# Moving work between the engines' orders at three stage boundaries of a two-block kernel, with part of a mask copied by ScalarE

## The reference, cut to what matters

```python
def even_layer(h, ...):
    u = rmsnorm(h, norm_g)
    z_a, xs, Bm, Cm, dt_f, dt_b, z_b, glu_v, glu_g = split_cols(u @ w_in, IN_E_SIZES)
    y_a = ssd_mixer(xs, Bm, Cm, dt_f, dt_b, z_a, ...)
    y_b = conformer_conv(glu_v, glu_g, dw_w, dw_b, ln_g, ln_b) * silu(z_b)
    return h + concatenate([y_a, y_b]) @ w_out

# ssd_mixer: xs, B, C go through a 5-tap convolution and silu; then in each direction
#   y = (C B^T * exp(differences of cumulated log a), lower triangle) @ (x * dt)
# then y_f + y_b + D * x, times silu(z_a), rmsnorm
```

## Time and profile before

| | us |
|---|---|
| median of 3 runs | 2369.8 |
| lowest, highest | 2365.5, 2371.14 |
| the profiled execution | 2370.42 |
| its span, first to last instruction | 2368.7 |
| mean granted clock of TensorE in it | 0.987 |
| busy: TensorE, VectorE, ScalarE, GpSimd | 2292.1, 1568.5, 1091.0, 453.4 |

### The profile page before, as it was taken

One profiled execution on the slowest core, in us unless ns is written; L12 is line 12 of the kernel. 1 busy time (PEld: TensorE's weight loads), 2 busy tenths in 40 slices (PEclk: granted clock), 3 DMA queues, 4 the chain that ended last, 5 costly groups with the idle time before them and its releaser, 6 DMA issues.

```text
span 2368.7 us, 43312 instructions
## 1 busy us (share of the span) xinstructions
PE 2292.1 (97%) x18679; PEld 2211.6 (93%) x18679; DVE 1568.5 (66%) x2517; ACT 1091.0 (46%) x1572; POOL 453.4 (19%) x315
## 2 busy tenths in 40 slices
PE   6999999999999999999999899988999999999998
PEld 6999999999999999999999788988999998888998
DVE  3546666554565567599999899895846456666564
ACT  4334555544544455344334565453535344444443
POOL 6210000000000000078877001750000012221000
PEclk9999999999999999999999999999999999999999
DMA  7756444555565565545556355564555565555552
GB/s 230 179 109 164 147 147 147 176 169 182 174 189 185 184 190 162 162 147 163 178 176 190 117 173 163 156 206 126 178 171 167 175 181 143 169 156 157 184 185 95
DMA packets 378894, 393.99 MB, mean 166 GB/s; under 512 B 12677, under 2 KB 371589, under 8 KB 378261
## 3 DMA queue, kind: packets, MB, share of 16 engines
q1 hardware_dynamic: 373984, 383.22, 53.2%
q0 software_dynamic: 2976, 6.63, 1.9%
q10 hardware_dynamic: 1744, 1.38, 0.2%
HBM read 388.85 MB, written 5.95 MB: 167 GB/s over the span
## 4 chain that ended last, share of the span: by engine, by line
PE 86%; DVE 10%; ACT 1%; issue 1%; DMA 1%; POOL 0%; SPq 0%; ACTq 0%; DVEq 0%
PE ps L421 26%; PE ps L423 25%; PE ps L422 25%; DVE ps L1704 3%; PE ps L2470 1%; PE ps L2399 1%; PE ps L2447 1%; PE ps L2459 1%; DVE wlo L374 1%; PE ps L2213 1%; DMA raw<-in_w_in_dram 1%; PE ps L2230 1%; PE ps L2132 1%; DVE arena L1672 0%; DVE op_lo L500 0%
## 5 line engine op out<-in xcount | busy, mean ns | idle before, releaser
L421 PE MATMUL ps<-op_hi,whi 128*128 128x256 f32 (+1 forms) x5440 | 1572.7, 289 | 12.5 <-POOL wlo L374 6.7
L423 PE MATMUL ps<-op_hi,wlo 128*128 128x256 f32 (+1 forms) x5440 | 1554.1, 286 | 0.0
L422 PE MATMUL ps<-op_lo,whi 128*128 128x256 f32 (+1 forms) x5440 | 1551.6, 285 | 0.0
L367 ACT ACTIVATE whi<-raw 128x1024 fp32r<-128x1024 f32 (+1 forms) x688 | 721.9, 1054 | 920.3 <-PE ps L423 893.2
L421 PEld LDWEIGHTS ps<-op_hi,whi 128*128 128x128 f32 x5440 | 1030.4, 189 | 37.4 <-issue 32.3
L423 PEld LDWEIGHTS ps<-op_hi,wlo 128*128 128x128 f32 x5440 | 1031.0, 190 | 0.0
L422 PEld LDWEIGHTS ps<-op_lo,whi 128*128 128x128 f32 x5440 | 1028.9, 189 | 0.4
L374 DVE TENSOR_TENSOR wlo<-raw,whi 128x1024 fp32r<-128x1024 f32 x552 | 669.0, 1227 | 497.1 <-ACT whi L367 496.3
L374 POOL TENSOR_TENSOR wlo<-raw,whi 128x1024 fp32r<-128x1024 f32 x136 | 334.5, 2471 | 1092.6 <-ACT whi L367 1092.2
L1704 DVE SCALAR_TENSOR_TENSOR ps<-arena,param_cols,ps 128x257 f32<-128x257 f32 (+6 forms) x448 | 183.4, 488 | 0.5
L752 POOL TENSOR_TENSOR arena<-arena 128x256 f32<-128x256 f32 x64 | 62.6, 998 | 277.8 <-DMA arena<-bias_by_column 277.8
(11 more groups left out here) (361 smaller groups left out, 1489.2 us busy)
## 6 DMA issues: line engine op xcount, KB each, us to landing
raw<-in_e_w_in_dram SPq DMA_DIRECT2D x96, 1024.0 KB, 5.4
raw<-in_w_in_dram SPq DMA_DIRECT2D x84, 1024.0 KB, 5.2
raw<-in_o_w_in_dram SPq DMA_DIRECT2D x64, 1024.0 KB, 6.1
raw<-in_e_w_out_dram SPq DMA_DIRECT2D x32, 1024.0 KB, 5.4
raw<-in_w_out_dram SPq DMA_DIRECT2D x16, 1024.0 KB, 5.3
raw<-in_w_ple_gate_dram SPq DMA_DIRECT2D x16, 1024.0 KB, 5.3
raw<-in_o_w_out_dram SPq DMA_DIRECT2D x16, 1024.0 KB, 5.3
arena<-cum_rows SPq DMA_DIRECT2D x16, 544.0 KB, 6.4
```

What stands on the lines that cost most here:

```text
L367: nc.scalar.activation(half_view(whi[c % 2], c, n), half_view(raw[c % RING], c, n), ACT.Copy).then_inc(hi_ready, 1)
L421: nc.tensor.matmul(o, wh, xh, start=(i % cpp == 0 and k == 0), stop=False)
L422: nc.tensor.matmul(o, wh, xl, start=False, stop=False)
L423: mm = nc.tensor.matmul(o, wl, xh, start=False, stop=(i % cpp == cpp - 1 and k == 7))
```

## The change

Three places in the order of the engines' work are changed, and two computations of the scan are written another way.

- bc to zb2: ScalarE does the last Silu of C and the first half of the next split ahead of the first two seg_exp. VectorE does seg(0), half of a split, the masks, seg(1), both weighs, the other half, seg(2).
- z2 to oa: VectorE does `ya_lo(0)` before z2's last pair, then the last product, `ya_lo(1)`, and the split of oa's chunk 1 after all four groups; `conv31(15, 2)` comes after the sums. ScalarE does the last `ya_hi` before the last squares.
- In oa: `total_pe` comes after chunk 1 in place of 0, `cf_sum` after 2 in place of 1, the totals of squares after chunks 5 and 7 in place of 3 and 5, and the steps behind shift by a chunk. `ya_scale` goes into the first `oa_add`.
- `masked_cb` keeps only the six products. The five copies are made by ScalarE (`cb_rest`), which waits for them (`cb_masked`); the first weigh of each group waits for the copies (`cb_rest`).
- The exponents of the meta positions of both directions are made by one tensor_tensor add at the beginning of seg and one tensor_tensor min at its end, on a strided view (`meta_ends`), in place of two tensor_scalar. The columns move for it.

```diff
@@ -116,7 +116,7 @@
...
 SSD_COLS = [(0, 0, 0, T2, 528), (0, 1, P, T2, 384), (1, 0, 0, P, 256), (1, 1, 0, 2 * P, 0),
-            (1, 2, 0, T2, 800), (0, 2, 2 * P, T2, 1072)]
+            (1, 2, 0, T2, 816), (0, 2, 2 * P, T2, 800)]
 META_CUT = 512 - T2
@@ -256,6 +256,10 @@
...
         XNAT = ar(q, 3, S1)
+
+        def meta_ends(sg):
+            return sg[0:META, 800:1088].rearrange("p (a n) -> p a n", n=META)[:, 0:18:17, :]
+
         assert q + 768 <= 19264
@@ -1044,17 +1048,29 @@
...
                 nc.scalar.activation(sg[:, 0:P], rw[:, 1, 0:P], ACT.Exp, bias=LNB[:, 1, SH + n:SH + n + 1])
-                nc.scalar.activation(sg[0:META, 800:1056], rw[0:META, 1, 0:2 * P], ACT.Exp, bias=LNB[0:META, 2, SH + n:SH + n + 1])
-                ins = nc.scalar.activation(sg[0:META, 1056:1088], sg[0:META, 1056:1088], ACT.Exp)
+                nc.scalar.activation(sg[0:META, 816:1072], rw[0:META, 1, 0:2 * P], ACT.Exp, bias=LNB[0:META, 2, SH + n:SH + n + 1])
+                ins = nc.scalar.activation(meta_ends(sg), meta_ends(sg), ACT.Exp)
                 ins.then_inc(S("seg_exp"), 1)
-            seg_exp(0)
-            seg_exp(1)
+            def cb_rest(G):
+                act.wait_ge(S("cb_masked"), G + 1)
+                for d, st, lo, hi, at in SSD_COLS[0:4]:
+                    r = (lo + P, hi) if d == 0 else (lo, P * st)
+                    if r[0] < r[1]:
+                        nc.scalar.activation(CBM[:, at + r[0] - lo:at + r[1] - lo], ps[:, 6 + st, r[0]:r[1]], ACT.Copy)
+                at = SSD_COLS[4][4]
+                nc.scalar.activation(CBM[0:META, at + META_CUT:at + 2 * P], ps[0:META, 7, T2:T2 + 2 * P - META_CUT], ACT.Copy)
+                nc.scalar.activation(CBM[0:META, at:at + META_CUT], ps[0:META, 6, T2:T2 + META_CUT], ACT.Copy).then_inc(S("cb_rest"), 1)
+
             act.wait_ge(acc_free, ST["zb2"].p0)
...
             s = ST["zb2"]
-            halves(act, "act", s.c0 + 2)
+            split_hi(act, s.c0 + 2, 0)
+            seg_exp(0)
+            cb_rest(0)
+            seg_exp(1)
+            split_hi(act, s.c0 + 2, 1)
@@ -1081,6 +1097,8 @@
...
                     seg_exp(2 * pr + 2)
+                if pr % 2 == 1 and pr < 2 * SG - 1:
+                    cb_rest(G + 1)
             act.wait_ge(acc_free, ST["z2"].p0)
@@ -1107,17 +1125,17 @@
...
             side("z2", z2_evac, pre=z2_pre, extra=zb2_silu)
+            ya_hi(2, ST["z2"].end)
+            ya_hi(3, ST["z2"].end)
             ya_square(6)
             ya_square(7)
-            ya_hi(2, ST["z2"].end)
-            ya_hi(3, ST["z2"].end)
             cf = NORM["cf"]
...
             def cf_steps(i):
-                if i == 0:
+                if i == 1:
                     act.wait_ge(S("factor_ms"), 5)
                     nc.scalar.activation(YRS, YRS, ACT.Sqrt).then_inc(S("factor_rt"), 1)
-                i -= 1
+                i -= 2
                 if i in (1, 3):
@@ -1798,16 +1816,21 @@
...
                     dve.wait_ge(S("y_psum"), n - 2 + SEED)
-                for d, st, lo, hi, at in SSD_COLS:
-                    m = P if st < 2 else META
+                both = [w[0:META, 2, :].rearrange("p (d h) -> p d h", d=2)[:, :, n:n + 1].to_broadcast([META, 2, META]) for w in (LNB, LND)]
+                v.do(V.tensor_tensor(meta_ends(SEG[n % 3]), ROWS[0:META, h // 2, :, h % 2, 2 * P:T2], both[0], ALU.add))
+                for d, st, lo, hi, at in SSD_COLS[0:4]:
+                    m = P
                     f = (P * st, P * st + m) if hi - lo > P + META else (lo, hi)
                     col = SH * d + n
-                    ins = V.tensor_scalar(SEG[n % 3][0:m, at + f[0] - lo:at + f[1] - lo], ROWS[0:m, h // 2, d, h % 2, f[0]:f[1]],
+                    V.tensor_scalar(SEG[n % 3][0:m, at + f[0] - lo:at + f[1] - lo], ROWS[0:m, h // 2, d, h % 2, f[0]:f[1]],
                                           LNB[0:m, st, col:col + 1], LND[0:m, st, col:col + 1], ALU.add, ALU.min)
-                ins.then_inc(S("seg_ready"), 1)
+                v.sync()
+                V.tensor_tensor(meta_ends(SEG[n % 3]), meta_ends(SEG[n % 3]), both[1], ALU.min).then_inc(S("seg_ready"), 1)
...
                 dve.wait_ge(S("seg_exp"), n + 1)
+                if n % 4 == 0:
+                    dve.wait_ge(S("cb_rest"), n // 4 + 1)
                 for m, lo, hi in ((P, 0, 800), (META, 800, 1088)):
@@ -1830,22 +1853,19 @@
...
                         o = T2 - META_CUT
-                        if d == 1:
-                            v.do(V.tensor_copy(CBM[0:n, at:at + META_CUT], ps[0:n, 6, T2:T2 + META_CUT]))
-                            v.do(V.tensor_copy(CBM[0:n, at + META_CUT:at + 2 * P], src[:, o + META_CUT:o + 2 * P]))
-                    elif hi - lo > n:
-                        r = (lo + n, hi) if d == 0 else (lo, P * st)
-                        v.do(V.tensor_copy(CBM[0:n, at + r[0] - lo:at + r[1] - lo], src[:, r[0]:r[1]]))
                     dlo = P * st
...
                 v.sync()
+                dve.sem_inc(S("cb_masked"), 1)
             seg(0)
+            split_lo(dve, "dve", ST["zb2"].c0 + 2, 0)
+            masked_cb(0)
             seg(1)
-            halves(dve, "dve", ST["zb2"].c0 + 2)
+            weigh(0)
+            weigh(1)
+            split_lo(dve, "dve", ST["zb2"].c0 + 2, 1)
             seg(2)
-            masked_cb(0)
-            weigh(0)
             for pr in range(2 * SG):
@@ -1854,7 +1874,8 @@
...
                     split_lo(dve, "dve", ST["zb2"].c0 + pr + 3, 0)
-                weigh(2 * pr + 1)
+                if pr > 0:
+                    weigh(2 * pr + 1)
                 if pr < 2 * SG - 1:
@@ -1876,19 +1897,27 @@
...
                     sum_pair(dve, 0, i // 2 - 2, T2)
-                if i == 15:
-                    ya_lo(0)
-                    ya_lo(1)
-
-            def conv_z2(i):
-                if i < 15:
+
+            s = ST["z2"]
+            for i in range(15):
+                z2_pre(i)
+                halves(dve, "dve", s.c0 + i + 2)
+                if i % 2 == 1:
+                    pair_wait(dve, s, i // 2)
+                    z2_times(i // 2, (s.p0 + i // 2) % 2)
+                if i < 14:
                     conv31(12 + i // 4, i % 4)
-
-            side("z2", z2_times, extra=conv_z2, pre=z2_pre)
+            ya_lo(0)
+            pair_wait(dve, s, 7)
+            z2_times(7, (s.p0 + 7) % 2)
+            ya_lo(1)
+            sum_pair(dve, 0, 5, T2)
             ya_lo(2)
             ya_lo(3)
+            halves(dve, "dve", s.end + 1)
             sum_pair(dve, 0, 6, T2)
             sum_pair(dve, 0, 7, T2)
+            conv31(15, 2)
@@ -1898,6 +1927,8 @@
...
             def oa_add(j, par):
+                if j == 0:
+                    ya_scale()
                 V.tensor_tensor(YT, ps[:, pairof(par), 0:T2], YRS.unsqueeze(1).to_broadcast([P, 2, T2]), ALU.mult).then_inc(acc_free, 1)
@@ -1913,11 +1944,10 @@
...
                 if i == 0:
-                    ya_scale()
                     conv31(15, 3)
...
                     dve.sem_inc(S("conv31_state"), 1)
-                i -= 1
+                i -= 2
                 if i == 1:
@@ -1929,7 +1959,7 @@
...
                     cf_half(1)
-                if i == 3:
+                if i == 4:
                     cf_half(2)
@@ -2406,12 +2436,12 @@
...
                 stream_pe(pe, "oa", NT=T2, need="ya", lo=i, hi=i + 1)
-                if i == 0:
+                if i == 1:
                     total_pe(pe, 0, 4, T2)
-                if i == 1:
+                if i == 2:
                     pe.wait_ge(S("conv31_state"), 2)
                     T.matmul(ps[:, 5, 0:T2], ones[:, :], CSUM[:, :], start=True, stop=True).then_inc(S("cf_sum"), 1)
-                for g in {3: (0, 1), 5: (2, 3)}.get(i, ()):
+                for g in {5: (0, 1), 7: (2, 3)}.get(i, ()):
                     pe.wait_ge(norm_half, 4 * cf + g + 1)
```

## The result

The changed kernel takes 2343.5 us (median of four runs, 2343.3 to 2344.1) beside 2367.7 us for the kernel before (four runs, 2365.2 to 2371.1). The ratio is 0.990, with a 95% interval of 0.988 to 0.991. The forecast was 2350.5 with a range from 2344 to 2360: the sign was right, the gain was 24 us by these medians where 19.3 was forecast, and the time fell half a microsecond outside the range. Against the profiled execution of before on which the sum was made, 2370.42 us, the changed kernel's 2343.57 is 26.9 us less. I account for these 26.9. A spell of half clock is a stretch in which TensorE's granted clock is 0.50.

The account below looks back on a forecast made before the run. TensorE, carrying 86% of the chain, was taken as the bound, so only its waits and low clock could pay. 7.3 - 0.8 + 12.8 = 19.3 us off 2369.8 gave 2350.5 us, range 2344 to 2360.

Parts of the forecast that it names:

- the rounds: Scan's seven four-head rounds after the first, 19.15 us each: copies' chain through ScalarE costs +0.12 us a round, 0.8 lost.
- Joint 1: Entry into the scan: with the Silu first, TensorE starts the first B-C product 7.1 us sooner; 7.3 us in all.
- what is late next: Entry of the scan: after the Silu, the wait on conv31_state, so TensorE starts at 1321.1 instead of 1328.2.
- The second term: Entry of the scan: 0.2 us gained from a shorter stay at the low clock.
- -0.8: Seven scan rounds: 0.8 us lost, bounds 0 to 3.5 us lost.
- Joint 2: From scan to z2: only its clock time changes; zero change taken, bounds -3.9 and +2 us.
- Rival B: Scan to z2: weigh runs before GpSimd's split, saving 2.1 us of stall and 1.8 of half clock; 2346.6 us, chance 0.17.
- the prediction's own objection to B: Scan to z2: the seg behind the weigh may be held by GpSimd's split instead.
- Joint 3: From z2 to oa: two more chunks done before the total of squares, 11.9 us plus 0.9, together 12.8 us.
- the 0.9 us that the chain was to give: In oa: VectorE has the sum of squares ready at 1624.3 where it was ready at 1625.2.
- the prediction's own signs of being wrong: Scan rounds' period above 19.7 us, or two chunks not won from z2 to oa.
- rival A: Copies' chain costs its upper end, 3.5 us, and z2 to oa gives only 8: gain 11, 2359 us, chance 0.17.

Follow-up runs that it names:

- meta_only: Kernel before with only the meta exponents of both directions made in two tensor operations, masks' copies still on VectorE, old order: 2367.1 us, ratio 0.999.
- copies_only: Kernel before with only the masks' five copies moved to ScalarE, meta exponents and order as before: 2370.6 us, ratio 1.000.
- before_again: The kernel before, unchanged, run once more for a second trace: 2368.0 us.
- joint1_only: Kernel before with only the new order at the entry of the scan (Silu first), masks' copies and meta exponents as before: 2361.9 us, ratio 0.997.
- joint3_only: Kernel before with only the new order from z2 to oa and the totals one or two chunks later: 2355.6 us, ratio 0.994.
- order_only: Kernel before with only VectorE's and ScalarE's new order from z2 to oa, TensorE's totals in their old places: 2370.1 us, ratio 1.001.
- shift_only: Kernel before with only the totals and their steps one or two chunks later in oa, order of z2's end as before: 2358.9 us, ratio 0.995.
- scan_only: Kernel before with both scan edits, copies by ScalarE and meta exponents in two operations, entry in the old order: 2364.2 us, ratio 0.998.
- tab_late: Changed kernel with GpSimd's table load moved behind z2's chunk 3: 2340.8 us, ratio 0.988 of before.
- ya_first: Changed kernel with ya_lo(1) ahead of z2's last pair: 2344.6 us, ratio 0.989 of before.
- best: Changed kernel with GpSimd's table load behind z2's chunk 3 and the masks' copies back on VectorE: 2340.4 us, ratio 0.988 of before.
- fill_last: Kernel before with seven idle products put in front of the last round's transposes, where TensorE waited: 2366.3 us.

## Why the prediction was right and wrong

The time fell outside the range mainly because two terms of the sum were wrong in kind: the rounds, taken to be bound by TensorE, and the half clock around the scan's last round, put at zero change.

**Joint 1** was right in its term (7.1 us, to 0.1) and in what is late next, the convolution. The second term, 0.2 us for the clock, was too small: the first rows ran faster and the stall of the second group shrank, 0.9 us more.

**The rounds** are the step that failed in its mechanism: "where it is negative TensorE is the bound and nothing is gained". I took TensorE to be the bound at 19.15 us since it was busy 19.97 of 20 us and showed no wait. It was not. The chain through VectorE, which I had set out with a slack of 0.05 us, was the bound, by 0.15 us a round, in pieces too small to be listed as waits; meta_only and copies_only show it from both sides. The larger piece stands at the y product. A weigh and the y product that uses it, before and after:

```profile
1376.50 1.34 DVE L1813 TENSOR_TENSOR arena<-arena 128x800 f32<-128x800 f32 x2
...
1377.98 2.25 PE L2399 MATMUL ps<-arena 128*64 128x272 f32 x24
```

```profile
1367.32 1.34 DVE L1836 TENSOR_TENSOR arena<-arena 128x800 f32<-128x800 f32 x2
...
1368.97 2.25 PE L2429 MATMUL ps<-arena 128*64 128x272 f32 x24
```

Before, the product starts 0.14 us after the weigh's end and 0.32 after the last multiplication; after, 0.31 and 0.22. So 0.10 us was VectorE's there, and 0.05 at the transposes, which started 0.05 us after y_tile's end and now start 0.17 after it. The terms were nearly right: masks and copies took 1360.00 to 1362.04, 2.04 us against 1.96 (forecast 2.03 at the low end), a seg 1.23 against 1.44 (a saving of 0.2 where I took 0.15). But two segs, not one, stand ahead of the y product that ends last, and a shorter chain pays. So -0.8 was +1.05. The copies took 0.81 us, from 1361.12 to 1361.93, and weigh started 0.11 later; the rows had given 0.84. My estimate of 1.01 us from the Trainium skill, ScalarE: Activation LUTs, section What ACT_TABLE_LOAD costs, is 0.20 above the measurement.

**Joint 2** had the largest error for its size: "I leave it at zero change". Its waits did stay (1.90 and 1.87 us against 2.06 and 1.86). Rival B came half true: the weigh does run first, at its usual 1.35 us, but GpSimd's split then holds the seg behind it, as the prediction's own objection to B had it, and the stall stays. In the kernel before, too, such a split held a seg, 3.74 us from 1457.39 for six operations that take 1.51 in other rounds. But the 3.0 us of half clock that followed the two waits in the profiled execution were not a fixed part of the kernel. In all seven traces with a last-round wait of 2.06 us or more (before, before_again, joint1_only, joint3_only, copies_only, order_only, shift_only) a spell followed; in the six with 1.6 to 1.9 us (after, scan_only, meta_only, tab_late, ya_first, best) none did. That is a count and no rule: behind GpSimd's wait of 1.9 us, the same in all, the spell came in seven of twelve traces (before, joint3_only, shift_only, scan_only, meta_only, ya_first, fill_last) and not in five (before_again, joint1_only, copies_only, order_only, after). I had bounded the term by -3.9 us, but gave that corner only to rival B, with a chance of 0.17, and only together with the stall.

**Joint 3** was right in mechanism and, partly by luck, nearly in size: 13.4 us to the total of squares against 12.8. TensorE waited 2.2 us there, as forecast (about 2). But VectorE's chain had the sum ready 46.1 us after z2's last multiplication, where I had worked out 44.9; before, it was 45.8. So of the 0.9 us that the chain was to give nothing came. It was paid back by the half clock behind line 2417 in before, which I expected to remain: after a wait of 2.2 us in place of 8.3, the total took 1.74 us to the next multiplication in place of 3.4. shift_only and order_only show that the two chunks are the gain, and that the new order is only what lets it be had.

So of the 7.6 us by which the forecast fell short of the profiled pair, 1.9 are the rounds, 3.0 the clock behind joint 2, 1.5 the clock and the chain at joints 1 and 3, and the rest, about 1, the stretches that the change doesn't touch.

Neither of the prediction's own signs of being wrong came: the period did not exceed 19.7 us, and two chunks were won at joint 3. Both were signs of a smaller gain, and the miss lay on the other side. One slip stands in rival A: 7.3 - 3.5 + 8 is 11.8 us and 2358.0, not 11 and 2359. It moves neither the forecast nor the range.

What decides between 2365 and 2370 us for one execution of before is only partly settled. In the traces most of such a step is the spell near 146 us, far ahead of the change: 3.3 to 4.8 us between the stretches that have it in full and those without it. Why it comes in some executions, with TensorE busy throughout, stays open.

## What to carry to other kernels

An engine that is busy 99.9% and shows no wait can still be held by a chain through another: sum the chain round by round and compare with the engine's own work, and test by shortening one link and lengthening another. Moving work off a busy engine gained nothing in these rounds, because the work stayed in the same chain. When a consumer waits for a chain, move the place where it asks before reordering the chain, and check what else is asked for in between. Where an edit touches only a part of the kernel, compare traces from the last event ahead of it, so that what happens before it does not count as gain or loss.

## What the runs showed of the chip

A wait costs more than itself when half clock follows: the last round's 2.06 us wait was followed by 5.35 us where 3.77 were needed, 1.6 us more, and seven idle products in its place removed it. Equal waits of 1.86 us were followed by such a spell in one execution of the kernel before and not in the other, so a sum that takes the clock from one profiled execution needs 1.6 us of margin for each short wait. That is the price at this place, where TensorE has work without a break behind the wait.

Half clock also came without a wait: near 146 us TensorE was busy 20.00 of 20 us and ran at half clock for 6.8 us in eight of 14 traces, 3.4 us in two and not at all in four.

A split of 128 x 1024 on GpSimd held VectorE operations that run beside it: a weigh took 3.58 us in place of 1.35, an addition on 16 x 32 elements 2.36 us in place of 0.17. Where the split ran before the weigh began, the weigh was held; where it began 0.93 us after the weigh had started, the seg behind it was.
